# Residual additions of the feed-forward chunks moved from VectorE to a ScalarE copy and an accumulating transfer

## The reference, cut to what matters

```python
D_MODEL = 2048; SEQ = 256; D_FF = D_FF_2 = 5632
# first block
h = rmsnorm(x, norm_ffn)
x = x + (silu(h @ w_gate) * (h @ w_up)) @ w_down
x = rmsnorm(x, norm_final)
# second block
h2 = rmsnorm_2(x, ffn_norm_w)
up = causal_dwconv(h2 @ w_ffn_up, conv_w, conv_b)   # 3 taps along the tokens
a, b = split(up, 2)
x = x + (silu(a) * b) @ w_ffn_down
x = rmsnorm_2(x, final_norm_w)
```

## Time and profile before

| | |
|---|---|
| median of 3 runs | 2567.9 us (2567.16 to 2567.9) |
| the profiled execution | 2567.3 us, span 2565.7 us, mean granted clock 0.997 |
| PE busy | 2526.1 us, 98% of the span |
| VectorE (DVE) busy | 1843.5 us, 72%; nine tenths or more in nine of the last ten of 40 slices |
| ScalarE (ACT) busy | 1300.5 us, 51% |
| POOL busy | 6.2 us |
| DMA | 480.50 MB, mean 187 GB/s |
| chain that ended last | PE 95%, ACT 2%, DVE 2%, issue 1% |
| L1440 w_lo (VectorE) | 508 times, 2.29 us each |
| L1013 w_hi (ScalarE) | 508 times, 1.92 us each |
| L1467 residual additions (VectorE) | 120 times, 1.22 us each |

### The profile page before, as it was taken

The page is one execution under the profiler, slowest core; times in us unless marked ns, Lnnn a source line. Parts: engine busy times, 40 slices in busy tenths (PEclk is TensorE's granted clock), DMA queues, the critical chain, the costliest instruction groups (busy, mean ns, idle before and its releaser), DMA issues.

```text
span 2565.7 us, 28052 instructions
## 1 busy us (share of the span) xinstructions
PE 2526.1 (98%) x11526; PEld 2089.5 (81%) x11526; DVE 1843.5 (72%) x1526; ACT 1300.5 (51%) x1240; POOL 6.2 (0%) x15
## 2 busy tenths in 40 slices
PE   8999999999999999999999999999999999999998
PEld 7888888788888888888888888888888888888886
DVE  5565577788888888867544554554789999999996
ACT  6544555444455444545444554333565555555554
POOL 0000000000000000000000000000000000000000
PEclk9999999999999999999999999999999999999999
DMA  8455446655555555555545555565556555555552
GB/s 282 157 168 193 136 148 214 210 189 192 196 197 191 190 193 190 187 189 197 174 156 195 170 169 192 191 197 195 175 202 205 195 195 196 195 195 194 193 194 96
DMA packets 239615, 480.50 MB, mean 187 GB/s; under 512 B 7632, under 2 KB 7760, under 8 KB 239232
## 3 DMA queue, kind: packets, MB, share of 16 engines
q1 hardware_dynamic: 238496, 474.10, 55.1%
q0 software_dynamic: 992, 4.60, 0.5%
HBM read 476.57 MB, written 2.10 MB: 187 GB/s over the span
## 4 chain that ended last, share of the span: by engine, by line
PE 95%; ACT 2%; DVE 2%; issue 1%; DMA 0%; SPq 0%; DVEq 0%; ACTq 0%
PE acc L609 24%; PE acc L613 24%; PE acc L611 24%; PE misc L609 6%; PE misc L613 6%; PE misc L611 6%; PE misc L642 2%; ACT w_hi L1013 2%; DVE x L1467 1%; DVE hid L1798 0%; PE misc L726 0%; PE misc L706 0%; DMA x<-in_x 0%; PE misc L720 0%; DVE w_lo L1440 0%
## 5 line engine op out<-in xcount | busy, mean ns | idle before, releaser
L1440 DVE TENSOR_TENSOR w_lo<-w_raw,w_hi 128x2048 fp32r<-128x2048 f32 x407 | 929.4, 2287 | 364.0 <-ACT w_hi L1013 362.5
L1013 ACT ACTIVATE w_hi<-w_raw 128x2048 fp32r<-128x2048 f32 x407 | 778.7, 1916 | 494.9 <-PE acc L613 378.0
L609 PE MATMUL acc<-w_hi,xt_hi 128*128 128x512 f32 x1456 | 576.9, 396 | 3.6 <-ACT hid L1016 3.3
L613 PE MATMUL acc<-w_hi,xt_lo 128*128 128x512 f32 x1456 | 568.4, 390 | 0.0
L611 PE MATMUL acc<-w_lo,xt_hi 128*128 128x512 f32 x1456 | 567.7, 390 | 0.0
L609 PEld LDWEIGHTS acc<-w_hi,xt_hi 128*128 128x128 f32 x1456 | 273.9, 188 | 62.6 <-ACT hid L1016 3.7
L613 PEld LDWEIGHTS acc<-w_hi,xt_lo 128*128 128x128 f32 x1456 | 273.8, 188 | 58.1
L611 PEld LDWEIGHTS acc<-w_lo,xt_hi 128*128 128x128 f32 x1456 | 274.1, 188 | 55.4
L1440 DVE TENSOR_TENSOR w_lo<-w_raw_more,w_hi 128x2048 fp32r<-128x2048 f32 x101 | 230.9, 2286 | 76.2 <-ACT w_hi L1013 75.8
L1013 ACT ACTIVATE w_hi<-w_raw_more 128x2048 fp32r<-128x2048 f32 x101 | 193.5, 1916 | 148.4 <-PE acc L613 79.0
L609 PE MATMUL misc<-w_hi,xt_hi 128*128 128x512 f32 x640 | 250.0, 391 | 0.0
(11 more groups left out here) (264 smaller groups left out, 3080.7 us busy)
## 6 DMA issues: line engine op xcount, KB each, us to landing
w_raw<-in_w_in SPq DMA_DIRECT2D x136, 1024.0 KB, 5.1
w_raw<-in_w_ffn_up SPq DMA_DIRECT2D x60, 1024.0 KB, 5.0
w_raw<-in_w_up SPq DMA_DIRECT2D x33, 1024.0 KB, 5.1
w_raw<-in_w_out SPq DMA_DIRECT2D x32, 1024.0 KB, 5.1
w_raw<-in_w_down SPq DMA_DIRECT2D x30, 1024.0 KB, 7.2
w_raw_more<-in_w_ffn_up SPq DMA_DIRECT2D x28, 1024.0 KB, 5.1
w_raw<-in_w_ffn_down SPq DMA_DIRECT2D x28, 1024.0 KB, 6.5
w_raw<-in_w_gate SPq DMA_DIRECT2D x27, 1024.0 KB, 5.2
```

Source lines behind the costliest of these rows:

```text
L609: nc.tensor.matmul(bank, hi[:, j, :], w_hi[:, t % RING, j, :], start=first and j == 0, stop=False, skip_group_check=shared)
L613: end = nc.tensor.matmul(bank, lo[:, j, :], w_hi[:, t % RING, j, :], start=False, stop=last and j == C - 1, skip_group_check=shared)
L1013: nc.scalar.activation(w_hi[:, t % RING], raw_tile(steps[t].slot), ACT.Copy).then_inc(hi_ready, 1)
L1440: nc.vector.tensor_tensor(w_lo[:, t % RING], raw_tile(steps[t].slot), w_hi[:, t % RING].bitcast(F32), ALU.subtract).then_inc(lo_ready, 1)
```

## The change

In the iterations 1 to 10 of both blocks the residual addition of D0 to D3 is no longer a VectorE instruction. ScalarE copies the pair of banks into one of two new tiles (`stage`; staged1 or staged2, alternating), which releases the pair, and POOL's queue issues a transfer that adds the tile to x in SBUF (`residual`, with `accum_op`), 80 in all. ScalarE's copy waits until the transfer of two steps earlier has landed. The last four additions of each block stay on VectorE, and the first of them waits for all transfers of the block (`all_added`).

In the first block, silu_gate moves from P2 and P4 to P4 and D0, gated_sums from D0 to D1 ahead of the split there, and hid_hi(0) from P5 to U2, behind the reading of P5. The reading of P1 waits for hid_ready (the product is written) instead of hid_turned (it is transposed).

In the second block conv_a and conv_b are put where u_a and u_b are, and staged2 takes their old places. The product is written over conv_b instead of conv_a. The readings of P1 and P5 into u_a and u_b wait for prod_done and h2_ready (product and residue of the iteration before) instead of the transposes, and move on ScalarE: P1's to k = 3, P5's to k = 4 ahead of the split.

The load of the first final_row moves on POOL's queue from the start of the first block to its end, behind the transfers, since staged1 lies on its place.

```diff
@@ -346,6 +346,7 @@
     s1_hi = place("s1_hi", [P, 4, C, P], F32R, ph + 16 * KB)
     s1_lo = place("s1_lo", [P, 4, C, P], F32R, ph + 24 * KB)
     raw_more = place("w_raw_more", [P, RAW_SLOTS - RING, C, N], F32, ph + 40 * KB)
+    staged1 = [place(f"staged1_{k}", [P, TOK, N], F32, ph + (32 + 4 * k) * KB) for k in range(2)]
     a_sum = place("a_sum", [P, 2 * C, S], F32, ph + 40 * KB)
     s_sum = place("s_sum", [P, 4, C, P], F32, ph + 48 * KB)
 
@@ -379,8 +380,9 @@
     h2_lo = place("h2_lo", [P, C, S], F32R, ph + 4 * KB)
     u_a = place("u_a", [P, TOK, N], F32, ph + 8 * KB)
     u_b = place("u_b", [P, TOK, N], F32, ph + 12 * KB)
-    conv_a = place("conv_a", [P, C, S], F32, ph + 16 * KB)
-    conv_b = place("conv_b", [P, C, S], F32, ph + 20 * KB)
+    conv_a = place("conv_a", [P, C, S], F32, ph + 8 * KB)
+    conv_b = place("conv_b", [P, C, S], F32, ph + 12 * KB)
+    staged2 = [place(f"staged2_{k}", [P, TOK, N], F32, ph + (16 + 4 * k) * KB) for k in range(2)]
     s2_hi = place("s2_hi", [P, 4, C, P], F32R, ph + 24 * KB)
     s2_lo = place("s2_lo", [P, 4, C, P], F32R, ph + 32 * KB)
     h2_last_hi = place("h2_last_hi", [P, C, S], F32R, ph + 24 * KB)
@@ -493,6 +495,7 @@
     dve_link = sem("dve_link")
 
     hid_ready = sem("hid_ready")
+    staged_added = [sem("staged0_added"), sem("staged1_added")]
     sum_ready = sem("weight_sum_ready")
     s_sum_ready = sem("s_sum_ready")
     s_hi_done = sem("s_hi_done")
@@ -586,13 +589,27 @@
         load(mult_a[:], ins["mult_a"], tables_loaded)
         load(taps[:], ins["taps"], tables_loaded)
 
-        pool.wait_ge(tile_used, FFN1_T + 1)
+        def residual(ffn, i, n):
+
+            m = 4 * (nth(ffn, i) - 1) + n
+            group_read(pool, (f"ffn{ffn}_down", i - 1, n))
+            pool.dma_start(x[:, :, n * N:(n + 1) * N], (staged1 if ffn == 1 else staged2)[m % 2][:],
+                           accum_op=ALU.add).then_inc(staged_added[m % 2], 16)
+
+        for i in range(1, NF):
+            for n in range(Q):
+                residual(1, i, n)
+        pool.wait_ge(lo_ready, more_free[1] + 1)
+        for k in range(2):
+            pool.wait_ge(staged_added[k], 16 * 2 * nth(1, NF - 1))
         load(final_row[:], ins["norm_final"].partition_broadcast(P), row_loaded)
-        pool.wait_ge(lo_ready, more_free[1] + 1)
         load(decay[:], ins["decay"], tables2_loaded)
         load(rope_r[:], ins["rope_r"], tables2_loaded)
         load(causal[:], ins["causal"], tables2_loaded)
 
+        for i in range(1, NF):
+            for n in range(Q):
+                residual(2, i, n)
         pool.wait_ge(tile_used, iteration_t(2, NF - 1) + order_of(2, NF - 1).index("P4") + 1)
         load(final_row[:], ins["final_norm_w_2"].partition_broadcast(P), row_loaded)
 
@@ -1223,16 +1240,24 @@
 
             scale = rstd[:, 1 if ffn == 1 else 4, :]
             if name == "P1":
-                act.wait_ge(tile_used, t + 1)
-                act.wait_ge(hid_turned if ffn == 1 else ua_turned, i)
+                act.wait_ge(tile_used, iteration_t(ffn, i) + order_of(ffn, i).index("P1") + 1)
+                act.wait_ge(hid_ready if ffn == 1 else prod_done, i)
                 copy(dst_a[:, 0, :], acc[:, 0, 0, :], scale[:, 0:1]).then_inc(p1_copied, 1)
             if name == "P5":
-                act.wait_ge(tile_used, t + 1)
-                act.wait_ge(hid_turned if ffn == 1 else ub_turned, i)
+                act.wait_ge(tile_used, iteration_t(ffn, i) + order_of(ffn, i).index("P5") + 1)
+                act.wait_ge(hid_turned if ffn == 1 else h2_ready, i)
                 copy(dst_b[:, 0, :], acc[:, 0, 1, :], scale[:, 0:1]).then_inc(p5_copied, 1)
             if name == "P7":
                 act.wait_ge(tile_used, t + 1)
                 copy(dst_a[:, 1, :], acc[:, 0, 0, :], scale[:, 1:2]).then_inc(p7_copied, 1)
+
+        def stage(ffn, i, t, n):
+            key = (f"ffn{ffn}_down", i - 1, n)
+            m = 4 * (nth(ffn, i) - 1) + n
+            act.wait_ge(tile_used, t + 1)
+            if m > 1:
+                act.wait_ge(staged_added[m % 2], 16 * (m // 2))
+            copy((staged1 if ffn == 1 else staged2)[m % 2][:], acc[:, pair_of(key)]).then_inc(pair_read[pair_of(key)], 1)
 
         def s_hi_piece(ffn, dst):
             act.wait_ge(s_sum_ready, ffn)
@@ -1254,13 +1279,15 @@
             for k, name in enumerate(order_of(1, i)):
                 t = iteration_t(1, i) + k
                 split(t + LEAD)
-                if i == 1 and name == "P5":
+                products_read(1, i, t, name, gate, hid)
+                if i == 1 and name == "U2":
                     hid_hi(0)
-                products_read(1, i, t, name, gate, hid)
-                if name == "P2":
+                if name == "P4":
                     silu_gate(i, 0)
-                if name == "P4":
+                if name == "D0":
                     silu_gate(i, 1)
+                if name[0] == "D":
+                    stage(1, i, t, int(name[1]))
                 if i == NF - 1 and name == "D1":
                     hid_hi(i, ht_last_hi)
                 if i < NF - 1 and name == "D3":
@@ -1353,7 +1380,7 @@
 
         def product_hi(i, dst=h2_hi):
             act.wait_ge(prod_done, i + 1)
-            copy(dst[:], conv_a[:]).then_inc(h2_hi_done, 1)
+            copy(dst[:], conv_b[:]).then_inc(h2_hi_done, 1)
 
         for k in range(8):
             t = FFN2_T + k
@@ -1381,13 +1408,20 @@
                     silu_a(i)
                 if i == NF - 1 and name == "D3":
                     product_hi(i, h2_last_hi)
+                if k == 4:
+                    products_read(2, i, t, "P5", u_a, u_b)
                 split(t + LEAD)
                 if k == 0 and i == 1:
                     last_tap(0, 1, conv_b)
                 if k == 2:
                     act.wait_ge(tile_used, iteration_t(2, i))
                     product_hi(i - 1)
-                products_read(2, i, t, name, u_a, u_b)
+                if k == 3:
+                    products_read(2, i, t, "P1", u_a, u_b)
+                if name == "P7":
+                    products_read(2, i, t, name, u_a, u_b)
+                if name[0] == "D":
+                    stage(2, i, t, int(name[1]))
                 if name == "P2":
                     last_tap(i, 1, conv_b)
                 if name == "D0":
@@ -1465,6 +1499,10 @@
             dve.wait_ge(tile_used, t + 1)
             xs = x[:, :, n * N:(n + 1) * N]
             nc.vector.tensor_tensor(xs, acc[:, pair], xs, ALU.add).then_inc(pair_read[pair], 1)
+
+        def all_added(ffn):
+            for k in range(2):
+                dve.wait_ge(staged_added[k], 16 * 2 * nth(ffn, NF - 1))
 
         def gain_quarter(q):
 
@@ -1821,14 +1859,12 @@
         for i in range(1, NF):
             for k, name in enumerate(order_of(1, i)):
                 t = iteration_t(1, i) + k
+                if name == "D1":
+                    gated_sums(i)
                 split(t + LEAD)
                 if i == 1 and name == "U2":
                     hid_lo(0)
                 results_read(1, i, t, name, gate, hid)
-                if name == "D0":
-                    gated_sums(i)
-                if name[0] == "D":
-                    add_group(t, ("ffn1_down", i - 1, int(name[1])))
                 if i == NF - 1 and name == "D1":
                     hid_lo(i, ht_last_hi, ht_last_lo)
                 if i < NF - 1 and name == "D3":
@@ -1836,6 +1872,8 @@
         for k in range(4):
             t = ROUND_T[4] - 4 + k
             split(t + LEAD)
+            if k == 0:
+                all_added(1)
             add_group(t, ("ffn1_down", NF - 1, k))
             if k > 0:
                 xt_lo_piece(2, k - 1)
@@ -1940,11 +1978,11 @@
             dve.wait_ge(silu_done, i + 1)
             for b in (2, 3):
                 bank_read(dve, ("ffn2b", i), b)
-            nc.vector.tensor_tensor(conv_a[:], conv_a[:], conv_b[:], ALU.mult).then_inc(prod_done, 1)
+            nc.vector.tensor_tensor(conv_b[:], conv_a[:], conv_b[:], ALU.mult).then_inc(prod_done, 1)
 
         def product_lo(i, hi=h2_hi, lo=h2_lo):
             dve.wait_ge(h2_hi_done, i + 1)
-            nc.vector.tensor_tensor(lo[:], conv_a[:], hi[:].bitcast(F32), ALU.subtract).then_inc(h2_ready, 1)
+            nc.vector.tensor_tensor(lo[:], conv_b[:], hi[:].bitcast(F32), ALU.subtract).then_inc(h2_ready, 1)
 
         for k in range(8):
             t = FFN2_T + k
@@ -1982,8 +2020,6 @@
                     taps_on(i, 1, conv_b)
                 if i < NF - 1 and name == "D1":
                     taps_on(i, 0, conv_a)
-                if name[0] == "D":
-                    add_group(t, ("ffn2_down", i - 1, int(name[1])))
         for k in range(4):
             t = STEPS - 4 + k
             split(t + LEAD)
@@ -1992,6 +2028,8 @@
             else:
                 dve.wait_ge(sumsq_done, 40 + 2 * k)
                 gain_quarter(k - 1)
+            if k == 0:
+                all_added(2)
```

## The result

| | |
|---|---|
| median of 5 runs | 2606.1 us (2605.85 to 2608.32) |
| before, beside it, 5 runs | 2567.2 us (2565.69 to 2567.9) |
| ratio | 1.0155, 95% interval 1.0141 to 1.0169 |
| the profiled execution | 2606.1 us, span 2604.5 us, mean granted clock 0.989 |

A forecast was written before the change was run, and what follows sets the result against it. PE was taken as the bound, so only its gaps count: -20.9 first block, +37.8 new wait, +15.6 clock, +2 tail, +34.5 on 2567.3 us. Forecast 2602 us, range 2577 to 2623.

The forecast's parts named there:

- the rivals: Clock hardly falls, 2587, chance 0.14; transfers land late, about 2670, 0.10; no new wait, 2548, 0.10; a tie, 0.03.
- The nine waits: First block, PE ahead of D2: waits on D0's residual addition go, nine times 1.6 us, 14.4 us saved.
- the single one: First block, iteration 1, U2's second half: PE's wait for P5's copy goes, 6.0 us saved including slow clock.
- The new wait: Second block, iterations 2 to 10: U2's second half waits for P5's copy behind product_lo, nine times 4.2, 37.8 us.
- The 3.0 from the shared place: Second block: even if nothing else moved, P5's copy into u_b would end 3.0 us too late for U2's second half.
- The clock: Second block: half clock after six of the nine new gaps, 15.6 us, between 0 and 23.4.
- The transfers: Accumulating 512 KB transfers on POOL's queue take 6.5 us to land, between 5.1 and 7.4, loose cap 10.
- the price of issuing: Issuing a transfer costs POOL 0.53 us and no other engine anything.
- Cover of 9.8 us: ScalarE's copy for D2 or D3 needs the transfer of two steps earlier; it has 9.8 us to land unnoticed.
- The first block's end: all_added holds the last four additions until D3's transfer lands: 2 us more, between 0 and 6.
- "Buys nothing by itself": Second block: PE is busy throughout, so taking 4 x 1.2 us of additions off VectorE gains nothing.
- The sum: Whole kernel: -20.9 + 37.8 + 15.6 + 2 = +34.5 us on 2567.3, forecast 2602.

The follow-up runs named there:

- e6: Kernel before the change, with only P1's copy waiting for hid_ready and hid_hi(0) moved behind P5's copy: 2561.3 us, ratio 0.9978.
- e5: Kernel before the change, with only the first block's gate-order edits; all additions stay on VectorE, no copies or transfers: 2544.2 us, ratio 0.9912.
- e2: Changed kernel with the second block's additions back on VectorE, conv_a and conv_b still on u_a and u_b: 2594.0 us, ratio 1.0104.
- e9: Changed kernel with silu_a at D3 ahead of the copy out of D3's banks instead of behind it: 2596.0 us, ratio 1.0108.
- e3: Changed kernel with conv_b and the second staging tile in places of their own, so u_b's place isn't shared: 2546.3 us, ratio 0.9919.
- e4: Changed kernel with product_lo ahead of its step's split instead of behind it, shared place kept: 2547.1 us, ratio 0.9921.
- e10: Changed kernel with product_lo between the weight sum and the residue of its step's split: 2573.2 us, ratio 1.0027.
- e7: e4's kernel with the additions of D2 and D3 in the first block's last iteration back on VectorE: 2543.4 us, ratio 0.9908.
- e8: Changed kernel with the first block's additions on VectorE in e5's order, and e3's places in the second block: 2543.7 us, ratio 0.9909.
- e11: e8 with the second block's last D2 and D3 additions on VectorE and final_row issued ahead of the last two transfers: 2542.4 us, ratio 0.9905.
- e1: Kernel before the change, with the change applied in the first block only, the second block as before: 2550.2 us, ratio 0.9934.
- e12: e5's kernel run again unchanged, beside e11: 2544.9 us, ratio 0.9916.

## Why the prediction held

**The result** was 2606 where 2602 was forecast, inside the range, slower as expected. None of the rivals came.

**The nine waits and the single one.** 20.9 us were forecast and 22.6 came, counted from one turn of hid to the next: 8.0 in iteration 1 (to the turn of hid, with its gap, its slow clock and its first D2 wait), 1.77 in each of the eight after it, 0.5 in the last. e6 alone gives 5.9 for the single wait, against 6.0. Each iteration got shorter by 1.77, so the 1.6 was 0.17 short. The reason given was incomplete. The prediction read in the earlier trace rows that D3's residue and the gated product stood ahead of the addition and credited ScalarE's copy with the gain. It passed over the bracket in the first of these rows, 2.58 us of idle time until w_hi, and did not ask why w_hi was late. e5 shows that the moved silu_gate and product suffice. Whether the copy alone, with the old order, would have done it too wasn't tried.

**The new wait.** 4.2 us nine times were forecast, restart included. The waits are 4.0, and from the last matmul's start to the next one's it is 4.17 us more than usual: 37.5 in all, where 37.8 were forecast. The 3.0 from the shared place stands by itself (e2). Of the other 1.0, e9 shows that 0.9 goes when silu runs ahead of the copy, and so no longer between it and G2's w_hi. e3 and e4 remove the cause in two different ways and the gap with it. That iteration 1 of the block has no such wait held too, with more to spare than was counted: its order puts 96 matmuls ahead of U2's second half (G2 and G3 are 24 each), not 84.

**The clock** is the term that was mis-sized twice, in opposite directions: six falls of 2.6 us were forecast, nine came. The 2.6 held the first matmul behind the gap, and counted like that they cost 1.4 to 3.0 us each: 15.6 forecast, 20.4 measured. That six was taken and not two or nine was a guess between one gap that brought the clock down and eight that didn't.

**The transfers.** 6.5 us to landing were forecast and the median is 5.0, at the lower bound of 5.1. So the plain transfer's 5.1 was the nearer row. The rule that an add in the DMA path costs a second source read (the Trainium skill, "Collectives: The Full Stack", "The bandwidth ceiling") isn't visible in the landing of 512 KB here. A second read does fit what the DMA engines spend. POOL's queue had 4.60 MB and 0.5% of their time before, 2.8 us for each MB, and the weight loads' queue takes 3.0 (54.2% for 474.1 MB); the 42 MB that the change adds take 9.4%, 5.8 us for each MB. That these go from SBUF to SBUF is new too, so the addition alone isn't shown to be the cause. The formula of the Trainium skill, "DMA: Bandwidth & Descriptors", "Anatomy of one DMA", by which an estimate of 3.2 us was worked out, doesn't fit: the quickest of the 80 landed 4.96 us after its issue began. What was wrong is the price of issuing: 1.18 us on POOL, not 0.53. It costs little where the queue is empty. Cover of 9.8 us was enough for all 80; the longest took 9.2.

**The first block's end** is the step that was furthest off in proportion: +2 forecast, +4.8 measured, inside its bounds of 0 to 6. It was built on a landing of 6.5 us, and the one transfer that all else waits for took 9.3 us from its issue to the addition. e3, with the same code there, had 6.3 from issue to addition and an end of 44.4 us in place of 47.3, so 1.8 longer than before: with a landing near the forecast one the mechanism gives the forecast 2. e10 has the same 44.4. The cause of the late landing is open; it isn't in the second block's edits, which come later, and the four runs of e3, like those of e4, spread over 3.5 us. Two such ends would do that, but only one run of each has a trace.

**"Buys nothing by itself"** for VectorE's time in the second block is nearly right and not quite. The weight-load waits of the earlier trace rows, taken for harmless, cost PE 0.2 us an iteration, about 2 us in all: iterations take 64.38 us (all but one in e3 and in e4) in e3, e4, e7, e8 and e11, where the additions are off VectorE, and 64.60 in e1, e5, e6 and e12. Against the loss of 56.6 us that didn't matter.

**The sum**: block one -22.6 + 4.8, block two +56.6 (53.4 forecast; 37.5 of gaps and 20.4 of slow clock, less 2 of weight-load waits, make 56 of it), the rest of the kernel and its end less than 0.3, together 38.8 us of span. 2567.3 + 38.8 is 2606.1.

## What to carry to other kernels

When a change frees an engine by letting two tensors share a place, follow the new wait back to the last engine without idle time, and look for what could go ahead of the releasing instruction: here moving one 1.2 us instruction ahead of its step's split gave back 59 us, and the shared place stayed. Before moving work to another engine to end a wait, follow the idle time ahead of it through both queues; an instruction that waits for the other engine and stands ahead of that engine's own input makes them take turns, and here a reordering brought the whole gain of the first block and no transfer to wait for. Price a PE gap with the slow clock behind it: here gaps of 3 to 4 us brought some 2.3 us more each time the clock fell.
